# Projections that step through their token columns in blocks of 16, alternately from the two halves of the tokens

## The reference, cut to what matters

```python
h = rmsnorm(x, norm1_g[l])
(hg_q, hg_f, hg_i, hg_g, ml_qk, ml_v, ml_if, ml_o,
 mb_z, mb_xbc, mb_dt, gate_pre) = jnp.split(h @ w_in[l], split_at, axis=-1)
...
mixed = (gates[:, :, 0] * (y_hg @ w_br_hg[l])
         + gates[:, :, 1] * (y_ml @ w_br_ml[l])
         + gates[:, :, 2] * (y_mb @ w_br_mb[l]))
x = x + mixed @ w_out[l]

u = causal_dwconv(rmsnorm(x, norm2_g[l]) @ w_up[l], ffn_conv_w[l], ffn_conv_b[l])
u_g, u_v = jnp.split(u, 2, axis=-1)
x = x + (jax.nn.silu(u_g) * u_v) @ w_down[l]
...
proj = jnp.einsum('bsd,de->bse', h, w_in)      # second block
```

## Time and profile before

| What | us |
|---|---|
| median of three runs | 1526.86 (1526.29 to 1527.47) |
| profiled execution, first to last instruction | 1524.3 |
| TensorE matmul busy | 1511.6 (99%) |
| TensorE weight load busy | 1235.9 (81%) |
| VectorE busy | 810.1 (53%) |
| ScalarE busy | 734.0 (48%) |
| GpSimd busy | 663.5 (44%) |

### The profile page before, as it was taken

The page is one execution under the profiler, slowest core; times in us unless marked ns, Lnnn a source line. Parts: engine busy times, 40 slices in busy tenths (PEclk is TensorE's granted clock), DMA queues, the critical chain, the costliest instruction groups (busy, mean ns, idle before and its releaser), DMA issues.

```text
span 1524.3 us, 20905 instructions
## 1 busy us (share of the span) xinstructions
PE 1511.6 (99%) x7172; PEld 1235.9 (81%) x7172; DVE 810.1 (53%) x1389; ACT 734.0 (48%) x1176; POOL 663.5 (44%) x510
## 2 busy tenths in 40 slices
PE   7999999999999999999999999999999999999999
PEld 6888888888888888888878888888888887777777
DVE  5677778442346731677633445555542335756761
ACT  6667665424346532466554344444443344545551
POOL 5334333444544454343344444444455544434432
PEclk9999999999999999999999999999999999999999
DMA  6222222232222222222223333223223343222212
GB/s 245 83 70 81 72 70 71 95 97 86 94 83 70 69 97 96 83 70 83 70 84 97 97 97 97 96 96 96 96 97 110 101 136 103 83 94 94 83 57 96
DMA packets 39399, 140.87 MB, mean 92 GB/s; under 512 B 4312, under 2 KB 4824, under 8 KB 39328
## 3 DMA queue, kind: packets, MB, share of 16 engines
q1 hardware_dynamic: 37664, 134.89, 27.0%
q10 hardware_dynamic: 1664, 5.01, 0.9%
HBM read 137.76 MB, written 2.13 MB: 92 GB/s over the span
## 4 chain that ended last, share of the span: by engine, by line
PE 98%; DVE 1%; DMA 0%; issue 0%; ACT 0%; SPq 0%; DVEq 0%
PE bank L519 27%; PE bank L523 27%; PE bank L522 27%; PE bank L757 3%; PE bank L1045 3%; PE bank L630 1%; PE bank L784 1%; PE bank L964 1%; PE bank L954 1%; PE bank L945 1%; PE bank L683 0%; PE bank L598 0%; PE bank L1036 0%; PE bank L540 0%; PE bank L685 0%; PE bank L671 0%
## 5 line engine op out<-in xcount | busy, mean ns | idle before, releaser
L446 POOL TENSOR_TENSOR wl<-raw,wh 128x512 fp32r<-128x512 f32 x488 | 643.4, 1340 | 839.9 <-ACT wh L1088 828.0
L519 PE MATMUL bank<-hh,wh 128*128 128x512 f32 x832 | 330.8, 398 | 0.0
L523 PE MATMUL bank<-hh,wl 128*128 128x512 f32 x832 | 324.7, 390 | 0.0
L522 PE MATMUL bank<-hl,wh 128*128 128x512 f32 x832 | 324.2, 390 | 0.0
L519 PE MATMUL bank<-yh,wh 128*128 128x512 f32 x800 | 314.7, 393 | 0.3 <-issue 0.2
L1088 ACT ACTIVATE wh<-raw 128x1024 fp32r<-128x1024 f32 x241 | 253.0, 1052 | 123.7 <-DMA raw<-slabs 123.3
L523 PE MATMUL bank<-yh,wl 128*128 128x512 f32 x800 | 311.5, 389 | 0.0
L522 PE MATMUL bank<-yl,wh 128*128 128x512 f32 x800 | 311.5, 389 | 0.0
L523 PEld LDWEIGHTS bank<-hh,wl 128*128 128x128 f32 x832 | 156.2, 188 | 33.6
L519 PEld LDWEIGHTS bank<-hh,wh 128*128 128x128 f32 x832 | 156.3, 188 | 33.0 <-issue 1.8
L522 PEld LDWEIGHTS bank<-hl,wh 128*128 128x128 f32 x832 | 156.4, 188 | 31.3
(11 more groups left out here) (363 smaller groups left out, 2036.3 us busy)
## 6 DMA issues: line engine op xcount, KB each, us to landing
raw<-slabs SPq DMA_DIRECT2D x245, 512.0 KB, 3.5
xs<-x SPq DMA_DIRECT2D x4, 512.0 KB, 5.7
xT<-xt SPq DMA_DIRECT2D x4, 512.0 KB, 12.7
wb<-bias_scratch ACTq DMA_DIRECT2D x1, 1792.0 KB, 8.5
wb<-bias_scratch ACTq DMA_DIRECT2D x2, 896.0 KB, 4.5
out<-a_l SPq DMA_DIRECT2D x4, 256.0 KB, 4.8
out<-au SPq DMA_DIRECT2D x3, 256.0 KB, 2.0
con<-consts ACTq DMA_DIRECT2D x1, 767.0 KB, 7.0
```

The lines of the kernel that those rows point to most:

```text
L446: pool.tensor_tensor(slab(wl, i, half), slab(raw, i, half), slab(wh, i, half).bitcast(F32), ALU.subtract).then_inc(S["slab_split"], 1)
L519: mm(bank[:, :], wh[:, s, b, :], xh, start=first and i == 0, stop=False)
L522: mm(bank[:, :], wh[:, s, b, :], xl, start=False, stop=False)
L523: ins = mm(bank[:, :], wl[:, s, b, :], xh, start=False, stop=last and i == len(order) - 1)
```

## The change

A helper `woven` turns a row of 512 columns into a view with three dimensions: 16 blocks `n`, two halves `h`, 16 columns `c`. Walked in that order it gives columns 0 to 15, 256 to 271, 16 to 31, 272 to 287, and so on to 240 to 255, 496 to 511. `project` uses this view for the moving rows of all three matmuls and for the bank, so each product still lands in the column of its own token. Nothing else is edited. On every engine the program has the same instructions in the same order as before; on TensorE the 5424 matmuls of `project` carry `128x16x2x16` in place of `128x512`. The edit puts four lines ahead of `project`, so L519, L522 and L523 become L523, L526 and L527.

```diff
@@ -226,6 +226,10 @@
             if isinstance(f, int):
                 return buf[:, f, :]
             return buf[:, bass.ds(f, 1), :].rearrange("p a t -> p (a t)")
+
+        def woven(ap):
+
+            return ap.rearrange("p (h n c) -> p n h c", h=2, c=16)
 
         def turned(ap):
 
@@ -507,7 +511,7 @@
                         ready=(), order=(), lo=None, late=None):
 
                 t0 = j0 if t0 is None else t0
-                bank, s = acc[t0 % 2], j0 % 4
+                bank, s = woven(acc[t0 % 2][:, :]), j0 % 4
                 pe.wait_ge(S["slab_split"], lin(2 * (j0 + 1), it, 2 * k) if lo is None else lo)
                 if first:
                     wait(pe, acc_free[t0 % 2], lin(t0 // 2, it, k // 2))
@@ -515,12 +519,12 @@
                 for i, b in enumerate(order):
                     if ready:
                         pe.wait_ge(*ready[i])
-                    xh, xl = src[0][:, base + b, :], src[1][:, base + b, :]
-                    mm(bank[:, :], wh[:, s, b, :], xh, start=first and i == 0, stop=False)
+                    xh, xl = woven(src[0][:, base + b, :]), woven(src[1][:, base + b, :])
+                    mm(bank, wh[:, s, b, :], xh, start=first and i == 0, stop=False)
                     if late:
                         pe.wait_ge(*late)
-                    mm(bank[:, :], wh[:, s, b, :], xl, start=False, stop=False)
-                    ins = mm(bank[:, :], wl[:, s, b, :], xh, start=False, stop=last and i == len(order) - 1)
+                    mm(bank, wh[:, s, b, :], xl, start=False, stop=False)
+                    ins = mm(bank, wl[:, s, b, :], xh, start=False, stop=last and i == len(order) - 1)
                 if len(order) == n or last:
                     ins.then_inc(S["slab_used"], 1)
```

## The result

The changed kernel takes 1593.12 us (median of 4 runs, 1592.78 to 1594.21) against 1526.73 us for the kernel before in the same comparison (4 runs): a ratio of 1.0435, 95% interval 1.0423 to 1.0448. It is slower by 66.4 us, and outside the forecast range.

What follows compares the result with a forecast made beforehand. TensorE's `project` matmuls were taken to bound the kernel. 5424 x 31 breaks x 0 = 0 on the 1524.3 us span, plus 2.6 us to the timed median, gave 1526.9 us; range 1523 to 1545 us.

Steps and rivals of the forecast that it cites:

- What bounds the kernel: TensorE, never kept waiting once it runs: 5424 matmuls of `project` at 226.8 ns each, 1230 us, 81% of the span.
- Writing breaks: 31 breaks in each `project` matmul's walk of the bank: value taken nothing, upper price one cycle, 0.417 ns.
- Reading breaks: 31 breaks in each `project` matmul's walk of the moving rows: value taken nothing, upper price 0.417 ns each.
- h = 16: L630's fp32 matmuls with runs of 16 columns, 7 breaks each: four take 0.44 us, like four contiguous ones.
- The ruler: L630, fp32 matmuls, the trace's only ones with gaps in the moving rows; bounds a reading break at 0.17 ns.
- Rival 2: In `project`'s matmuls: a whole cycle lost at each reading or writing break, 70 us, 1597 us in all; chance 0.15.
- Rival 3: In `project`'s matmuls: faster by the fixed 13.3 ns each, in full 72 us, 1455 us; chance 0.07.
- Lines: SBUF reads of moving rows in 16-byte lines wanting two hits each: by this rule the change costs nothing.

Runs made afterwards that it cites:

- h = 32, c = 4: Changed kernel with runs of 4 columns taken from 32 places in turn, in place of runs of 16 from two: 1512.32 us, ratio 0.9907 to the kernel before.
- 2 x 64: Changed kernel with runs of 64 columns in place of 16, still from two halves: 1526.91 us, ratio 0.9999 to the kernel before.

## Why the prediction was wrong, point by point

- **What bounds the kernel**: right. TensorE is 98 to 99% of the chain on both sides, without waits, at a granted clock of 1.00 (the 2.4 GHz level), so 13.2 ns a matmul went to the end almost undiminished.
- **Writing breaks**: right at nothing (1.0001), although the rows behind it bounded the price only weakly. The strict rule of the Trainium skill (PSUM — Partial Sum Buffer, Specifications), that any non-contiguous pattern slows matmuls significantly, is not borne out for runs of 16 columns, the one length at which the bank was walked alone; with runs of 4 on both sides the kernel was faster than straight. The Trainium skill adds (Advanced Engine Details and Errata, PSUM Cachelines) that every two consecutive elements should be contiguous: all these walks keep to that, the dear runs of 2 too.
- **Reading breaks**: this is the step that failed, in its sentence "The nearest row is h = 16, with runs of the same length, so the value I take is nothing." That term of the sum was put at 0 and measured 13.2 ns a matmul. The ruler was read rightly: fp32 matmuls of the projections, with two cycles a column, show no price for runs of 4 to 32 columns and a small one for runs of 2, as L630 did. It doesn't carry over to fp32r at one column a cycle, where the same order costs 13.3 ns. I had named this unknown and weighed it at 0.15. The range was too narrow even by the ruler: its own bound of 0.17 ns a break allows some 28 us over 31 breaks, 1555 us, and the range ended at 1545.
- **Rival 2** is what happened by place (reading side) and by size: 1597 us forecast, 1593 measured. Its mechanism, one cycle at each break, is refuted all the same. 7 breaks cost nothing, 15 cost 10 ns, 63 cost 16.6, and with 384 columns 11 and 23 breaks cost the same. That 31 x 0.417 ns = 12.9 comes near the measured 13.2 is luck, a coincidence of this one walk.
- **Rival 3** was dismissed on the ground that nothing was left to save. That was wrong too: the 13.3 ns beside one cycle a column are not fixed. In straight walks they are 14.1 at 384 columns (174.1 - 160.0) and 16.0 at 448 (202.7 - 186.7), and h = 32, c = 4 has 10.1 of them at 512 (223.4 - 213.3).
- **Lines**: the two hits on a 16-byte line that the Trainium skill asks for (SBUF — State Buffer, on cachelines) agreed with the row at half rate. At full rate runs of 2 columns, two hits a line, cost 113 ns more at h = 2 and 204 to 260 more elsewhere. Both sides were walked so, and no run shows which of them costs it.

What stays open is the rule. Shown is that the price of the change belongs to the reader of the moving rows in fp32r, where one cycle goes to a column. For the other walks, with both sides alike, it is shown that the pace depends on run length, on the route (h), on the width and on the neighbour, and that two walks have two paces each, settled where a stretch begins. That their prices lie on the reading side as well is likely and not shown. Which property of the memory, of its reader or of the change from one matmul to the next makes 2 x 64 free, 2 x 16 dear and 32 x 4 better than straight, no run here shows.

## What to carry to other kernels

An access pattern with breaks that is free at half the engine's rate may not be free at the full rate: price it on the same type and rate, with one walk for a whole tile, since the start distances of mixed neighbours mislead. In a kernel bound by fp32r matmuls keep the moving rows in aligned runs of 64 columns or more (at 512 columns none of these walks cost over 2 ns), or try a few walks, because straight was not the quickest; the bank took runs of 16 columns at no price. And let a quick tile prove itself over the whole kernel: one walk with 220 ns in a tile ended at no gain, because most of its stretches settled at 230 ns; another with 224 ns kept 1%.

## What the runs showed of the hardware that I had not expected

- An fp32r matmul of 512 columns takes 226.7 ns from start to start, 13.3 above a cycle a column, and the order in which its rows are read moves this between 220 and 487 ns. In fp32, orders with h = 2 take 429 ns an instruction, 453 with runs of 2.
- One and the same walk can settle at either of two paces (220 or 231 ns; 223 or 227 ns), and no stretch of unbroken matmuls changed from one to the other.
- Steps move with the way the weights are read though the moving rows don't change: straight 226.7 ns, 229 with one weight column, 230 with 64 columns, 233 with every second (15.40 us for 66, in the run with the fp32 tiles).
